# Attention in eight groups of two row blocks, with the values in passes of 256 columns

## What is computed

```python
def forgetting_attention(q, k, v, log_f):
    s = q.shape[2]
    scale = q.shape[-1] ** -0.5
    cum = jnp.cumsum(log_f, axis=-1)
    outs = []
    for blk in range(s // Q_BLOCK):
        lo = blk * Q_BLOCK
        hi = lo + Q_BLOCK
        logits = (jnp.einsum("bhtd,bhsd->bhts", q[:, :, lo:hi], k[:, :, :hi]) * scale
                  + (cum[:, :, lo:hi, None] - cum[:, :, None, :hi]))
        mask = (lo + jnp.arange(Q_BLOCK))[:, None] >= jnp.arange(hi)[None, :]
        p = jax.nn.softmax(jnp.where(mask, logits, -jnp.inf), axis=-1)
        outs.append(jnp.einsum("bhts,bhsd->bhtd", p, v[:, :, :hi]))
    return jnp.concatenate(outs, axis=2)
```

## Time and profile before

| what | us |
|---|---|
| time, median of three runs | 776.29 (776.09 to 776.43) |
| time of the profiled execution | 776.31 |
| its span, first to last instruction | 774.5 |
| TensorE busy | 765.9 (99%) |
| VectorE busy | 373.0 (48%) |
| ScalarE busy | 257.4 (33%) |
| GpSimd busy | 24.0 (3%) |

### The profile page before, as it was taken

How to read it: one execution, slowest core, us unless ns; L and a number is a source line. 1 busy time by engine, 2 the same in 40 slices (tenths; PEclk the granted TensorE clock), 3 DMA queues, 4 the chain that set the end, 5 groups by cost and what they waited for, 6 DMA issues and landing times.

```text
span 774.5 us, 9676 instructions
## 1 busy us (share of the span) xinstructions
PE 765.9 (99%) x3927; PEld 631.2 (81%) x3927; DVE 373.0 (48%) x561; ACT 257.4 (33%) x423; POOL 24.0 (3%) x51
## 2 busy tenths in 40 slices
PE   9999999999999999999999999999999999999996
PEld 7988888888676888888879888888888888888885
DVE  5878544257977525335354444443333445223123
ACT  6454122344555323233243322322232322213121
POOL 5000000012000000000000000000000000000000
PEclk9999999999999999999999999999999999999999
DMA  8523333301111154133312422332233323322302
GB/s 247 149 97 110 108 105 122 100 14 43 56 55 57 55 173 153 55 109 108 111 53 82 137 87 76 109 109 80 83 110 109 109 90 116 120 68 85 121 1 108
DMA packets 61792, 75.11 MB, mean 97 GB/s; under 512 B 3682, under 2 KB 49842, under 8 KB 61748
## 3 DMA queue, kind: packets, MB, share of 16 engines
q1 hardware_dynamic: 61744, 74.50, 30.1%
q10 hardware_dynamic: 4, 0.00, 0.0%
HBM read 72.40 MB, written 2.10 MB: 96 GB/s over the span
## 4 chain that ended last, share of the span: by engine, by line
PE 72%; issue 1%; DVE 0%; ACT 0%; POOLq 0%; POOL 0%; ACTq 0%
PE bank L1235 23%; PE bank L1236 23%; PE bank L1237 23%; PE bank L1498 1%; PE bank L1460 1%; PE bank L1481 1%; PE bank L1467 0%; PE bank L1248 0%; PE bank L1464 0%; DVE w_lo L787 0%; ACT square_out L492 0%; ACT x L749 0%; DVE x L1207 0%; DVE work L953 0%; POOLq L153 0%
## 5 line engine op out<-in xcount | busy, mean ns | idle before, releaser
L787 DVE TENSOR_TENSOR w_lo<-stage,w_hi 128x1024 fp32r<-128x1024 f32 x125 | 152.5, 1223 | 233.7 <-ACT w_hi L511 225.0
L1235 PE MATMUL bank<-hT_hi,w_hi 128*128 128x512 f32 (+1 forms) x680 | 258.9, 381 | 0.6 <-DVE hT_lo L772 0.6
L1237 PE MATMUL bank<-hT_hi,w_lo 128*128 128x512 f32 (+1 forms) x680 | 256.2, 377 | 0.0
L1236 PE MATMUL bank<-hT_lo,w_hi 128*128 128x512 f32 (+1 forms) x680 | 256.2, 377 | 0.0
L511 ACT ACTIVATE w_hi<-stage 128x1024 fp32r<-128x1024 f32 x126 | 132.4, 1053 | 134.9 <-PE bank L1237 134.1
L1235 PEld LDWEIGHTS bank<-hT_hi,w_hi 128*128 128x128 f32 x680 | 128.0, 188 | 23.9 <-POOL w_lo L456 0.8
L1237 PEld LDWEIGHTS bank<-hT_hi,w_lo 128*128 128x128 f32 x680 | 127.9, 188 | 23.6
L1236 PEld LDWEIGHTS bank<-hT_lo,w_hi 128*128 128x128 f32 x680 | 128.1, 188 | 22.4
L1236 PE MATMUL bank<-w_lo,aT_hi 128*128 128x512 f32 x176 | 68.5, 389 | 0.0
L1235 PE MATMUL bank<-w_hi,aT_hi 128*128 128x512 f32 x176 | 68.5, 389 | 0.0
L1237 PE MATMUL bank<-w_hi,aT_lo 128*128 128x512 f32 x176 | 68.5, 389 | 0.0
(11 more groups left out here) (191 smaller groups left out, 737.9 us busy)
## 6 DMA issues: line engine op xcount, KB each, us to landing
stage<-in_w_in SPq DMA_DIRECT2D x21, 1024.0 KB, 5.2
stage<-in_w_gate SPq DMA_DIRECT2D x11, 1024.0 KB, 5.3
stage<-in_w_up SPq DMA_DIRECT2D x11, 1024.0 KB, 5.4
stage<-in_w_down SPq DMA_DIRECT2D x22, 512.0 KB, 4.4
stage<-in_w_out SPq DMA_DIRECT2D x4, 1024.0 KB, 5.0
x_nat<-in_x SPq DMA_DIRECT2D x4, 512.0 KB, 5.5
stage<-in_w_br_mlstm SPq DMA_DIRECT2D x4, 512.0 KB, 3.5
stage<-in_w_br_fox SPq DMA_DIRECT2D x4, 512.0 KB, 4.5
```

The lines of the kernel that those rows point to most:

```text
L787: dve.tensor_tensor(ring(w_lo, g), staged(g), ring(w_hi, g).bitcast(F32), ALU.subtract).then_inc(lo_split, 1)
L1235: pe.matmul(o, a_hi, b_hi, start=first, stop=False)
L1236: pe.matmul(o, a_hi, b_lo, start=False, stop=False)
L1237: return pe.matmul(o, a_lo, b_hi, start=False, stop=last)
```

## The change

The 16 steps become eight groups g of two steps each, 2g and 2g+1 (`FOX_GROUPS`). TensorE's order in a group: T(2g), the logits of 2g+2 without mask, T(2g+1), the logits of 2g+3 without mask, the masks of both, `FILL[g]` pieces, and one `fox_values(g)` for both row blocks. There a matmul has 256 moving columns (both blocks) where both see the key block, and 128 for the last key block. `pT` is laid out as [head, key block, 256 columns] and moves from the place of the work tiles to that of `q_m`. On VectorE and ScalarE the same operations are put in a new order, and the pieces, tanhs and splits are spread over the groups.

```diff
-        pT = at("pT", [P, 2, SEQ], F32, W)
+        pT = at("pT", [P, 2, ROWS, 2 * P], F32, R)
...
-            blocks = tile[:, :, 0:(q + 1) * P].rearrange("p h (j t) -> p h j t", t=P)
-            return blocks[:, :, :, low * HALF_ARRAY:(low + 1) * HALF_ARRAY]
+            t = (q % 2) * P + low * HALF_ARRAY
+            return tile[:, :, 0:q + 1, t:t + HALF_ARRAY]
...
-                if v >= 1:
-                    act.wait_ge(fox_pv, v)
+                if v >= 2:
+                    act.wait_ge(fox_pv, v // 2)
...
-            act.wait_ge(y_m, H_M)
-            for v in range(FOX_PAIRS):
-                if v >= ROWS and v % ROWS == 0:
-                    take_yfT_hi(v // ROWS - 1)
-                if v in TANH_AT:
-                    first_gate_tanh(TANH_AT.index(v))
-                fox_take_low(v)
-                if v == 0:
+            for g in range(FOX_GROUPS):
+                if g >= 2 and g % 2 == 0:
+                    take_yfT_hi(g // 2 - 1)
+                fox_take_low(2 * g)
+                if g in TANH_AT:
+                    first_gate_tanh(TANH_AT.index(g))
+                fox_take_low(2 * g + 1)
+                if g == 0:
                     take_ymT_hi(3)
-                if v in SPLIT_AT:
-                    split_hi(G_BR + AHEAD + SPLIT_AT.index(v))
-                if v + 2 < FOX_PAIRS:
-                    fox_softmax(v + 2)
+                if g + 1 < FOX_GROUPS:
+                    fox_softmax(2 * g + 2)
+                    fox_softmax(2 * g + 3)
+                if g in SPLIT_AT:
+                    split_hi(G_BR + AHEAD + SPLIT_AT.index(g))
...
-                if v == 0:
-                    dve.wait_ge(y_m, H_M)
-                if v >= 1:
-                    dve.wait_ge(fox_pv, v)
+                if v >= 2:
+                    dve.wait_ge(fox_pv, v // 2)
...
-            for v in range(FOX_PAIRS):
-                if v == 0:
+            for g in range(FOX_GROUPS):
+                fox_take_high(2 * g)
+                if g == 0:
                     open_gate(3)
-                fox_take_high(v)
-                if v == 0:
+                fox_take_high(2 * g + 1)
+                if g + 1 < FOX_GROUPS:
+                    fox_row_max(2 * g + 2)
+                    fox_row_max(2 * g + 3)
+                if g >= 2 and g % 2 == 0:
+                    take_yfT_lo(g // 2 - 1)
+                if g == 0:
                     ymT_product(3)
-                if v >= ROWS and v % ROWS == 0:
-                    take_yfT_lo(v // ROWS - 1)
-                if 1 <= v < FOX_PAIRS - 1:
-                    fox_divide(v + 1)
-                if v + 2 < FOX_PAIRS:
-                    fox_row_max(v + 2)
-                if v == 0:
+                if g + 1 < FOX_GROUPS:
+                    fox_divide(2 * g + 2)
+                if g == 0:
                     take_ymT_lo(3)
-                if v in SPLIT_AT:
-                    split_lo(G_BR + AHEAD + SPLIT_AT.index(v))
+                if g + 1 < FOX_GROUPS:
+                    fox_divide(2 * g + 3)
+                if g in SPLIT_AT:
+                    split_lo(G_BR + AHEAD + SPLIT_AT.index(g))
...
+
+            def fox_mask(v):
+                _, q = fox_pair(v)
                 for h2 in range(2):
-                    pe.matmul(banks[h2][:, q * P:n], ident_b[:, :], mask_b[:, :], start=False,
+                    pe.matmul(psum[logit_bank(2 * v + h2)][:, q * P:(q + 1) * P], ident_b[:, :], mask_b[:, :], start=False,
                               stop=True).then_inc(logits, 1)
...
-            def fox_values(v):
-
-                hp, q = fox_pair(v)
-                if v == 0:
+            def fox_values(g):
+
+                hp, q = fox_pair(2 * g)
+                q0 = q // 2 * 2
+                if g == 0:
                     pe.wait_ge(v_ready, 2 * ROWS)
-                for h2 in range(2):
-                    pe.wait_ge(fox_PT[h2], v + 1)
-                if v % ROWS == 0:
+                for low in range(2):
+                    pe.wait_ge(fox_PT[low], 2 * g + 2)
+                if g % 2 == 0:
                     take(FOX_Y, (yfT_lo_ready, hp + 1))
-                for j in range(q + 1):
+                for j in range(q0 + 2):
+                    t = P if j > q0 else 0
                     for h2 in range(2):
                         c = (2 * hp + h2) * DH_F
-                        last = pe.matmul(psum[FOX_Y][h2 * DH_F:(h2 + 1) * DH_F, q * P:(q + 1) * P],
-                                         v_f[:, j, c:c + DH_F], pT[:, h2, j * P:(j + 1) * P],
-                                         start=(j == 0), stop=(j == q))
+                        last = pe.matmul(psum[FOX_Y][h2 * DH_F:(h2 + 1) * DH_F, q0 * P + t:(q0 + 2) * P],
+                                         v_f[:, j, c:c + DH_F], pT[:, h2, j, t:2 * P],
+                                         start=(j == 0), stop=(j == q0 + 1))
                 last.then_inc(fox_pv, 1)
...
-            for v in range(FOX_PAIRS):
-                fox_transpose(v)
-                if v + 2 < FOX_PAIRS:
-                    fox_logits(v + 2)
-                if v == 0:
+            for g in range(FOX_GROUPS):
+                for n in range(2):
+                    fox_transpose(2 * g + n)
+                    if g + 1 < FOX_GROUPS:
+                        fox_logits(2 * g + 2 + n)
+                if g + 1 < FOX_GROUPS:
+                    fox_mask(2 * g + 2)
+                    fox_mask(2 * g + 3)
+                if g == 0:
                     mlstm_transpose(3)
-                for _ in range(FILL[v]):
+                for _ in range(FILL[g]):
                     gate_piece(next(pieces))
-                fox_values(v)
+                fox_values(g)
...
+FOX_GROUPS = FOX_PAIRS // 2
...
-SPLIT_AT = (1, 2, 6, 10)
-TANH_AT = (2, 6, 10)
-FILL = (3, 2) + (2,) * 6 + (2, 2, 1, 2, 2, 1, 1, 1)
+SPLIT_AT = (0, 1, 3, 5)
+TANH_AT = (1, 3, 5)
+FILL = (5, 4, 4, 4, 4, 3, 3, 2)
```

More of the change, by code:

```diff
@@ L373, in _ @@
                 if s == S_OUT - 4:
-                    sp.wait_ge(fox_pv, FOX_PAIRS)
+                    sp.wait_ge(fox_pv, FOX_GROUPS)
                     sp.wait_ge(num_m, 2 * H_M)
@@ L627, in take_yfT_hi @@
             def take_yfT_hi(hp):
-                act.wait_ge(fox_pv, ROWS * (hp + 1))
+                act.wait_ge(fox_pv, 2 * (hp + 1))
                 act.activation(yfT_hi[:, hp, :], psum[FOX_Y][:, :], ACT.Copy).then_inc(yfT_hi_ready, 1)
@@ L1129, in _ @@
                         if b == 0:
-                            dve.wait_ge(fox_pv, FOX_PAIRS)
+                            dve.wait_ge(fox_pv, FOX_GROUPS)
                         s = mix_sum[b % 2]
@@ L1523, in _ @@
             fox_logits(0)
+            fox_mask(0)
             mo_columns(3, 4, KD)
             fox_logits(1)
+            fox_mask(1)
             def gate_piece(i):
```

## The result

The changed kernel takes 782.85 us (median of five runs, 782.67 to 784.76) against 776.43 for the kernel before (776.09 to 776.61): the ratio is 1.0089, 95% interval 1.0074 to 1.0103. It is slower by 6.4 us; 6.0 were forecast, and 782.3 as the time.

The account below looks back on a forecast made before the run. TensorE was taken to set the pace, with VectorE right behind. Idle time 10.6 less 0.6 old waits less 4.0 saved gave +6.0; 774.5 + 6.0 + 1.8 = 782.3 us, likeliest 780.0 to 784.6, with rivals 779.6 to 785.4.

Parts of the forecast that it names:

- Prices on TensorE: Start-to-start costs of transposes, logits, masks, fills and values in the attention loop; new V 1.65 or 0.80 us.
- The choice of columns over instructions for V: In the values: cost follows columns passed, so 256-column passes gain 0; by instructions, at most 3.4 us in all.
- The tops: Fixed costs of V, fills and logits-to-mask switches on TensorE; fewer of them save 3.8 us, taken as 4.0.
- the old waits: Waits the loop already has before the change, 0.6 us, taken off the new idle time.
- the case without the waits: In the loop, only TensorE's saving of 4.0 us counts: 772.3 us; chance 0.09 for faster.
- The wait in each group: Ahead of T(2g+1), TensorE waits for VectorE's queued copy of T(2g) to `pT`; idle time 10.6 us in all.
- The two estimates: In VectorE's chain: 0.35 us from first mask to first maximum, 0.13 from copy's end to TensorE's start.
- Group 1: From masks at 202.84 to T(3): TensorE idle 0.15 + 0.4 + 2.4 = 2.9 us, waiting for divides and copy.
- the likeliest case: Whole kernel slower by a net 6.0 us, at 780.0 to 784.6 us; the forecast gives it 0.74.
- Rival B: After the first two stalls the granted clock halves; 3 us more taken, 785.3 us; chance 0.08.
- Rival A: In the loop, VectorE's chain is shorter than TensorE's, leaving only the saving: 772.3 us; chance 0.09 for faster.
- C: On TensorE, fixed costs stay or a 256-column pass costs more than two of 128: up to 1.5, 783.8 us; chance 0.04.

Follow-up runs that it names:

- the run with 128 columns: The changed kernel with each group's values in passes of 128 columns again, one row block after the other: 783.02 us.
- the late split: The changed kernel with VectorE's gate-granule split moved from the end of its group to behind the next group's first copy: 779.30 us.
- the short maximum: The changed kernel with the row maximum taken over the last key block of 128 columns only: 778.75 us.
- the moved pieces: The changed kernel with four of 29 fill pieces (groups 0 and 6) moved between the first logits and the second transposes: 783.42 us.
- the combined edits: The changed kernel with the mask behind each logits, first-step maxima between the copies, and splits behind the next group's first copy: 777.60 us.

## Why the prediction was right

**Prices on TensorE: right.** V 1.67 and 0.80 (1.65 and 0.80), a fill of four pieces with the masks 3.15 (214.25 to 217.40; 0.38 + 2.76 = 3.14). The choice of columns over instructions for V, made from the slope of the logits, is shown by the run with 128 columns. The tops were right too, but rounded up: 4.6 were taken off for them and the old waits, 4.3 in the trace. A saving on the engine that waits is no gain: the case without the waits, 772.3, was wrong by 10.

**The wait in each group: right,** in place, releaser and size, in seven of eight groups to 0.25 us; the late split and the short maximum show the chain, the moved pieces show that TensorE's idle time is its consequence. The two estimates it rested on, 0.35 from mask to maximum and 0.13 from copy to transposes, measured 0.27 and 0.06 in group 6; they are a bit large, and the few hundredths between neighbours in the queue make up for it.

**Group 1: the term differs in this profile,** 2.9 forecast, 1.3 measured. The start of T(3) was right to 0.1 us; the slow clock had filled part of the wait with slower work. At the full clock, in the run with 128 columns, the same term is 2.85: the chain was right, and what the likeliest case left out is the clock. The order of the events there, `ymT_product(3)` behind the maxima and ScalarE's exponentials behind it, was as described (ScalarE waits 3.81 for line 955).

**Rival B, the clock, happened beside the forecast, not in its place.** It had a chance of 0.08 as a case of its own at 785.3. The profile has two drops, one of them free, and its run took 784.76, near that case's time; the median of 782.85 is 0.5 above the forecast. The step that failed is to treat it as an alternative that always costs: the drop in the stretch where VectorE is the bound moved T(3) by less than 0.1 us, and the other one cost 1.5 us. Without the clock the terms as measured give nearly the forecast: idle time of 10.6 (the table, with 2.85 in group 1) less 4.3 is 6.3 where the forecast has 6.0, so 782.6. Whether the last 0.25 of the median is slow clock isn't shown.

**Rival A and C: not seen.** No transposes follow the logits at once, and the tops are gone, to within the 0.3 above. That the chain has to fall under TensorE's before the order pays is what the combined edits show: at 777.60 they are still above the kernel before.

## What to carry to other kernels

When steps are merged to save switches on the busiest engine, write down for every wait inside the merged step the whole queue of the engine that answers it, from the moment at which its inputs exist; the longer of the two chains sets the period, and time saved on the other one becomes idle time. Filling such idle time with other work gave nothing here; taking work out of the answering queue, moving it to where that engine waits itself, or letting it start earlier gave up to its full length (1.15 us for a split of 1.13 in group 6), as long as that queue was the longer chain. Merge what has no such wait (here the values; that paid only once VectorE's queue was in the order of need), and leave the steps that keep the second engine fed as fine as they were.

## What the runs showed of the hardware

The granted clock can fall after a stall is over. In the changed kernel TensorE was idle for most of 199.6 to 201.8, worked at 1.00 until 203 and then at 0.55 from 203 to 206, busy all the time; behind the stall of group 6 it was the same (1.00 to 251, 0.51 from 251 to 254). After the last matmul of the kernel before, by contrast, it fell with nothing running. The Trainium skill, TensorE: Matmul & The Clock Gate, Part 1, ties the low rate to idleness; the traces agree, but the drop lies behind the idle time, on work that was issued without a gap. It didn't come after each such stall: the kernel with the late splits has a stall of the same length in group 0 (1.97 us at 201.20) and keeps 1.00 there. The kernel with values of 128 columns has the stall of group 6 too (1.65 us at 250.94, 1.66 at 250.78 in the changed kernel) and keeps 1.00 from 251 to 254, but falls after the stall of group 1 (0.67 from 212 to 216). So the length of the last stall alone doesn't tell whether a drop follows.

Two heads' values in float32 cost 0.21 us for 128 columns of both, the same in 28 instructions as in 16; the weight loads between them, of which the 16 have 12 fewer, don't show.
